# Delta rule prepared under the last projection units, its rows broadcast through DRAM, memory attention woven into the chunk steps

## The reference, cut to what matters

```python
h = rms_norm(x, mix_norm[l]) @ a_w_in[i]
qkv, gate, b_raw, a_raw, q_mem = jnp.split(h, ...)
o_a = gated_deltanet(qkv, gate, b_raw, a_raw, ...)        # 6 heads of 128
o_m = memory_attention(q_mem, mem_n @ w_mem_kv[l])        # 4 heads of 64, 256 keys
x = x + jnp.concatenate([o_a, o_m], axis=-1) @ w_out[l]
# inside gated_deltanet, after conv + silu and the l2 norms of q and k:
g_cum = cumsum(g)                                         # per chunk, per head
decay = exp(g_cum[i] - g_cum[j]) where j <= i
t_mat = where(strict, (k * beta) @ k.T * decay, 0) + eye
u = solve(t_mat, v * beta);  w = solve(t_mat, k * beta * exp(g_cum))
qk = (q @ k.T) * decay
# then chunk after chunk:
v_new = u_c - w_c @ state
out = q_c @ state + qk_c @ v_new
state = state * d_c + k_c.T @ v_new
```

## Time and profile before

| | us |
|---|---|
| median of three runs | 1333.41 (1329.31 to 1335.06) |
| profiled execution | 1335.27 |
| its span | 1333.1 |
| PE busy in the span | 1278.9 (96%) |
| DVE busy | 889.4 (67%) |
| ACT busy | 710.4 (53%) |
| POOL busy | 83.8 (6%) |

### The profile page before, as it was taken

One profiled execution on the slowest core, in us unless ns is written; L12 is line 12 of the kernel. 1 busy time (PEld: TensorE's weight loads), 2 busy tenths in 40 slices (PEclk: granted clock), 3 DMA queues, 4 the chain that ended last, 5 costly groups with the idle time before them and its releaser, 6 DMA issues.

```text
span 1333.1 us, 26311 instructions
## 1 busy us (share of the span) xinstructions
PE 1278.9 (96%) x10172; PEld 1244.6 (93%) x10172; DVE 889.4 (67%) x1503; ACT 710.4 (53%) x1026; POOL 83.8 (6%) x88
## 2 busy tenths in 40 slices
PE   7999999999999999899999999799999899999997
PEld 7899999999999987898999999699999868999996
DVE  7576689766657966436766755766665666766644
ACT  6445656666546762344666544556544444756432
POOL 7270000000000000430000000000000000000000
PEclk9999999999999997698999999899999998999999
DMA  8535555555644431002555642455564312555630
GB/s 329 187 105 195 168 180 190 190 189 191 227 153 160 160 129 61 1 1 66 187 189 189 233 178 94 151 180 180 200 235 150 107 64 96 186 178 182 242 126 32
DMA packets 48396, 208.71 MB, mean 157 GB/s; under 512 B 3376, under 2 KB 5560, under 8 KB 43848
## 3 DMA queue, kind: packets, MB, share of 16 engines
q1 hardware_dynamic: 46992, 203.89, 44.2%
q10 hardware_dynamic: 1336, 3.89, 0.8%
HBM read 206.68 MB, written 1.09 MB: 156 GB/s over the span
## 4 chain that ended last, share of the span: by engine, by line
PE 90%; DVE 5%; ACT 2%; issue 2%; DMA 0%; POOL 0%; ACTq 0%; DVEq 0%
PE main L1591 27%; PE main L1593 27%; PE main L1592 27%; PE main L1963 3%; PE side L1673 1%; DVE w_lo L823 1%; PE main L1948 1%; PE side L1653 1%; PE side L2004 1%; PE main L1933 1%; PE side L1684 0%; PE main L1934 0%; PE main L2018 0%; PE side L1641 0%; ACT w_hi L447 0%
## 5 line engine op out<-in xcount | busy, mean ns | idle before, releaser
L1591 PE MATMUL main<-xg_hi,w_hi 128*128 128x256 f32 (+1 forms) x2024 | 573.2, 283 | 2.5 <-DVE w_lo L823 0.9
L1592 PE MATMUL main<-xg_hi,w_lo 128*128 128x256 f32 (+1 forms) x2024 | 570.9, 282 | 0.0
L1593 PE MATMUL main<-xg_lo,w_hi 128*128 128x256 f32 (+1 forms) x2024 | 570.5, 282 | 0.0
L447 ACT ACTIVATE w_hi<-raw 128x1024 fp32r<-128x1024 f32 (+2 forms) x364 | 404.6, 1114 | 302.9 <-PE main L1593 300.5
L823 DVE TENSOR_TENSOR w_lo<-raw,w_hi 128x1024 fp32r<-128x1024 f32 (+2 forms) x364 | 466.4, 1288 | 6.3 <-ACT w_hi L447 5.5
L1591 PEld LDWEIGHTS main<-xg_hi,w_hi 128*128 128x128 f32 x2024 | 383.3, 189 | 5.8 <-issue 1.7
L1593 PEld LDWEIGHTS main<-xg_lo,w_hi 128*128 128x128 f32 x2024 | 383.9, 190 | 0.0
L1592 PEld LDWEIGHTS main<-xg_hi,w_lo 128*128 128x128 f32 x2024 | 381.0, 188 | 0.5
L1591 PE MATMUL main<-h_hi,w_hi 128*128 128x256 f32 x704 | 198.1, 281 | 0.0
L1592 PE MATMUL main<-h_hi,w_lo 128*128 128x256 f32 x704 | 198.1, 281 | 0.0
L1593 PE MATMUL main<-h_lo,w_hi 128*128 128x256 f32 x704 | 198.1, 281 | 0.0
(11 more groups left out here) (360 smaller groups left out, 1516.1 us busy)
## 6 DMA issues: line engine op xcount, KB each, us to landing
raw<-in_w_gu_a SPq DMA_DIRECT2D x44, 1024.0 KB, 5.2
raw<-in_w_gu_b SPq DMA_DIRECT2D x44, 1024.0 KB, 5.2
raw<-in_w_down_a SPq DMA_DIRECT2D x16, 1408.0 KB, 5.8
raw<-in_w_down_b SPq DMA_DIRECT2D x16, 1408.0 KB, 5.9
raw<-in_w_in SPq DMA_DIRECT2D x20, 1024.0 KB, 5.3
raw<-in_w_in_a SPq DMA_DIRECT2D x13, 1024.0 KB, 5.2
raw<-in_w_up SPq DMA_DIRECT2D x4, 1024.0 KB, 5.1
raw<-in_w_out SPq DMA_DIRECT2D x4, 1024.0 KB, 5.2
```

What stands on the lines that cost most here:

```text
L447: act.activation(w_hi[:, u % RING, 0:n], raw[:, s % RAW, u % 2, 0:n], ACT.Copy).then_inc(hi_ready, 1)
L1591: pe.matmul(dst, a_hi, b_hi, start=first, stop=False)
L1592: pe.matmul(dst, a_lo, b_hi, start=False, stop=False)
L1593: return pe.matmul(dst, a_hi, b_lo, start=False, stop=last)
```

## The change

It does five things.

- `ba` is projected after turn 1; its Sigmoid, Exp and Ln lie in turns 3 and 4 of ScalarE, the scan in turn 6 of VectorE, its transpose in turn 7 of TensorE, the Sqrt of the norms in turn 15, the column scales in turn 16 of VectorE, with the turn into rows right behind unit 16 on TensorE.
- The 24 rows go to DRAM from ScalarE's queue in turn 17 and come back in turn 18 and after, 512 KB for each head, broadcast over the partitions (`spread_rows`), in place of `along_rows`.
- The grams of head h are made after unit 18 + h, into two side banks in turn. VectorE makes the decay of head h in turn 19 + h (`decays`) and `n_t`, `a_t` in turn 20 + h (`grams`); GpSimd multiplies by the broadcast rows.
- v is turned in turns 20 to 22 and scaled by ScalarE, k in turns 24 and 25.
- The four memory heads leave the projection loop and stand between the sets of the recurrence.

The products of the inversion, the streams of weights and everything outside layer A's mixer are unchanged. The diff, cut to these parts:

```diff
 # ScalarE
+                if t == 3:
+                    act.wait_ge(evac, BA_TILE + 1)
+                    act.activation(ba[0:6, :], ba[0:6, :], ACT.Sigmoid).then_inc(ba_act, 1)
+                    act.wait_ge(ba_dve, 1)
+                    link(act.activation(sp2[32:38, :], sp1[32:38, :], ACT.Abs))
+                if t == 4:
+                    act.activation(small[32:38, 30:31], par[32:38, C_ALOG:C_ALOG + 1], ACT.Exp).then_inc(ba_act, 1)
+                    link(act.activation(sp2[32:38, :], sp2[32:38, :], ACT.Exp, scale=-1.0))
+                    act.activation(sp2[32:38, :], sp2[32:38, :], ACT.Ln, bias=one_c[32:38, :]).then_inc(ba_act, 1)
...
+                if t == 15:
                     act.wait_ge(csum, 12)
...
+                if t == 17:
+                    act.wait_ge(rows_ready, 1)
+                    act.dma_start(delta_rows.rearrange("h (i n) -> (h i) n", i=4), head_rows[:, :]).then_inc(rows_out, 16)
+                if t == 18:
+                    act.wait_ge(rows_out, 16)
+                    for h in range(3):
+                        spread_rows(h)
+                if t >= 19 and t - 19 < DH:
+                    h = t - 19
+                    act.wait_ge(diff_ready, h + 1)
+                    act.activation(dec[:, h % 2, 0, :], dec[:, h % 2, 0, :], ACT.Exp).then_inc(decay_ready, 1)
+                    if 0 <= h - 1 and h + 2 < DH:
+                        act.wait_ge(dec_ready, h)
+                        spread_rows(h + 2)
+                if t >= 21 and t - 21 < 3:
+                    j = t - 21
+                    act.wait_ge(turned_v, j + 1)
+                    for i in range(4):
+                        h, c = 2 * j + i // 2, i % 2
+                        ins = act.activation(kqv[:, 12 + h, c * P:(c + 1) * P], side[2][:, i * P:(i + 1) * P],
+                                             ACT.Copy, scale=b_col[:, c, h:h + 1])
...
+            exps(MEM_A)
+            new_values(vn0, 0, 1)
+            new_values(vn0, 1, 2)
+            exps(MEM_A + 1)
+            copy_pt(MEM_A)
+            act.wait_ge(rec_dve, 4)
+            square_outputs(0)
+            exps(MEM_A + 2)
+            copy_pt(MEM_A + 1)
+            new_values(vn1, 0, 9)
+            new_values(vn1, 1, 10)
+            exps(MEM_A + 3)
+            copy_pt(MEM_A + 2)
             act.wait_ge(rec_dve, 12)
...
 # VectorE
             link(dve.memset(cx[:, :, 0:3], 0.0))
+            dve.wait_ge(small_hi, 2)
+            low(wba_lo[:, :], wba[:, :], wba_hi[:, :]).then_inc(small_lo, 1)
+
+            def decays(h):
+
+                r, d = h % 3, h % 2
+                dve.wait_ge(spread_in[r], 16 * (h // 3 + 1))
+                for c in range(2):
+                    dve.scalar_tensor_tensor(dec[:, d, 0, c * P:(c + 1) * P], spread[:, r, 1, c * P:(c + 1) * P],
+                                             g_col[:, c, h:h + 1], const[:, K_CAUS:K_CAUS + P],
+                                             ALU.subtract, ALU.add)
+                dve.tensor_tensor(g_last[:, h:h + 1], spread[:, r, 1, P - 1:P], g_col[:, 0, h:h + 1],
+                                  ALU.subtract).then_inc(diff_ready, 1)
+
+            def grams(h):
+
+                dve.wait_ge(dec_ready, h + 1)
+                dve.wait_ge(gram, h + 1)
+                for i, dst in enumerate((n_t, a_t)):
+                    for c in range(2):
+                        ins = dve.scalar_tensor_tensor(
+                            dst[:, 2 * h + c, :], side[h % 2][:, i * SEQ + c * P:i * SEQ + (c + 1) * P],
+                            kq_inv[:, c, h:h + 1], dec[:, h % 2, 1 + i, c * P:(c + 1) * P], ALU.mult, ALU.mult)
+                ins.then_inc(n_ready, 1)
 
             def convolve(t, taps):
...
+                if t == 16:
+                    dve.wait_ge(col_act, 2)
+                    link(dve.reciprocal(cols[:, 80:104], cols[:, 184:208]))
+                    k_beta, q_scale = packed[:, :, :, 0], packed[:, :, :, 2]
+                    dve.tensor_tensor(k_beta, kq_inv[:, :, 0:6], b_col, ALU.mult)
+                    dve.tensor_copy(packed[:, :, :, 1], g_col)
+                    link(dve.tensor_scalar(q_scale, kq_inv[:, :, 6:12], DK ** -0.5, None, ALU.mult))
+                    dve.tensor_tensor(packed[:, :, :, 3], q_scale, e_g, ALU.mult).then_inc(cpk_ready, 1)
+                    link(dve.tensor_tensor(k_neg, k_beta, e_g, ALU.mult))
+                    dve.tensor_scalar(k_neg, k_neg, -1.0, None, ALU.mult)
+                if t == 17:
+                    dve.wait_ge(rows_t, 1)
+                    dve.tensor_copy(head_rows[:, :], side[3][0:24, 256:512]).then_inc(rows_ready, 1)
+                if t >= 19 and t - 19 < DH:
+                    decays(t - 19)
+                if t >= 20:
+                    grams(t - 20)
+
...
+            row_maxima(MEM_A)
+            row_maxima(MEM_A + 1)
+            normalise(MEM_A)
+            for j in range(2):
+                by_heads(state, main[2 + j], j, 3 + j)
+            normalise(MEM_A + 1)
+            for j in range(2):
+                by_heads(o_a[:, :, 0:P], main[j], j, 5 + j)
+            row_maxima(MEM_A + 2)
...
 # GpSimd
+            for h in range(DH):
+                r, d = h % 3, h % 2
+                gp.wait_ge(decay_ready, h + 1)
+                if h >= 2:
+                    gp.wait_ge(n_ready, h - 1)
+                gp.tensor_tensor(dec[:, d, 1, :], dec[:, d, 0, :], spread[:, r, 0, :], ALU.mult)
+                gp.tensor_tensor(dec[:, d, 2, :], dec[:, d, 0, :], spread[:, r, 2, :], ALU.mult)
+                gp.wait_ge(gram, h + 1)
+                q_late = kqv[:, 6 + h, P:SEQ]
+                gp.tensor_tensor(q_late, q_late, spread[:, r, 3, P:SEQ], ALU.mult).then_inc(dec_ready, 1)
...
 # TensorE
+                if t == 1:
+
+                    bank = bank_of(BA_TILE)
+                    pe.wait_ge(small_lo, 2)
+                    for k in range(KC):
+                        w = slice(k * 38, k * 38 + P)
+                        ins = triple(bank[:, 0:SEQ], wba_hi[:, w], wba_lo[:, w], xs_hi[:, k], xs_lo[:, k],
+                                     k == 0, k == KC - 1)
+                    ins.then_inc(extra_done, 1)
                 if 3 <= t < 15:
...
+                if t == 7:
                     pe.wait_ge(ba_dve, 2)
...
+                if t == 16:
                     pe.wait_ge(cpk_ready, 1)
...
+                if t >= 18 and t - 18 < DH:
+
+                    h = t - 18
+                    if h >= 2:
+                        pe.wait_ge(n_ready, h - 1)
+                    for i, other in enumerate((h, 6 + h)):
+                        for c in range(2):
+                            ins = pe.matmul(side[h % 2][:, (2 * i + c) * P:(2 * i + c + 1) * P], kqv[:, h, chunks[c]],
+                                            kqv[:, other, chunks[c]], start=True, stop=True)
+                    ins.then_inc(gram, 1)
+                if t >= 20 and t - 20 < 3:
+
+                    j = t - 20
+                    if j == 0:
+                        pe.wait_ge(csilu, 18)
+                    else:
+                        pe.wait_ge(vt_done, j)
+                    for i in range(4):
+                        ins = pe.transpose(side[2][:, i * P:(i + 1) * P],
+                                           kqv[:, 12 + 2 * j + i // 2, i % 2 * P:(i % 2 + 1) * P], ident)
+                    ins.then_inc(turned_v, 1)
+                if t >= 24:
+
+                    j = t - 24
+                    pe.wait_ge(vt_done, 3)
+                    for i in range(3):
+                        ins = pe.transpose(side[2 + j][:, i * P:(i + 1) * P], kqv[:, 3 * j + i, 0:P], ident)
+                    ins.then_inc(turned_k, 1)
 
...
             pe.wait_ge(ident_ready, 1)
-            pe.wait_ge(rows_ready, 1)
-            chunks = (slice(0, P), slice(P, SEQ))
-            for h in range(DH):
-                for i, (r0, r1) in enumerate(((h, 6 + h), (12 + h, 18 + h))):
-                    bank = bank_of(t0 + 3 * h + i)
-                    along_rows(bank[:, 0:SEQ], r0)
-                    along_rows(bank[:, SEQ:2 * SEQ], r1).then_inc(spread, 1)
-                bank = bank_of(t0 + 3 * h + 2)
-                for i, other in enumerate((h, 6 + h)):
-                    for c in range(2):
-                        ins = pe.matmul(bank[:, (2 * i + c) * P:(2 * i + c + 1) * P], kqv[:, h, chunks[c]],
-                                        kqv[:, other, chunks[c]], start=True, stop=True)
-                ins.then_inc(gram, 1)
-            t0 = FIRST_TILE["kt"]
-            for j, (a, b) in enumerate(((0, 4), (4, 6))):
-                bank = bank_of(t0 + j)
...
 
-            pe.wait_ge(d_dve, 21)
-
-            each(main[0:2], [(lambda h: d_t[:, h, :], lambda h: kqv[:, 12 + h, 0:P])])
-
-            each(main[2:4], [(lambda h: k_dec[:, h, :], lambda h: vn0[:, h, :])],
+            scores(MEM_A)
+            scores(MEM_A + 1)
+
```

(31 more changed lines are left out.)

312 lines of the change are left out of this document (113 added, 199 removed).

## The result

The changed kernel takes 1347.7 us (median of four runs, 1345.22 to 1350.54) against 1331.83 us for the kernel before on the same chip: ratio 1.0119, 95% interval 1.0086 to 1.0151. It is slower, as forecast (1342; the range 1324 to 1356 holds it). The profiled execution is 1345.22 us (span 1343.4), 9.95 us above that of before; the medians lie 15.9 us apart.

The account below looks back on a forecast made before the run. TensorE's chain of waits was taken to bound the kernel. Removing 44.0 us and adding 34.0 under the projection, 8.5 in the recurrence and 10.4 for the clock gave +8.9: 1344.2 against the profile, 1342 against the median; range 1324 to 1356.

Parts of the forecast that it names:

- (c): Turn 1 of the projection: TensorE waits for `wba_lo`, made by VectorE behind a reciprocal; 1.4 us, between 0 and 2.4.
- (d): Turn 7: TensorE waits for the scan, late through ScalarE's five function switches; 4.4 us, and 0.3 for the transpose.
- (e): Turn 16: TensorE waits right behind unit 16 for VectorE's column scales; 4.3 us with the two transposes.
- (g): Turns 21 to 23: before each gram TensorE waits for VectorE's `n_ready` of head h - 2; 3.3 us each, 9.9 us.
- (h): Turn 20: TensorE's wait includes the DMA of the broadcast rows, taken as 4 us; 5.0 us, from 3.3 to 9.
- (i): Between the last unit and the inversion's first product: 8.5 us where 7.5 stood, 1.0 us more, from 0 to 3.
- (j): Recurrence: scores, transposes and outputs of the four memory heads, less filled idle time, plus new waits; 8.5 us added.
- (k): Low TensorE clock after the gaps of turns 7, 16 and 20 to 24: 10.4 us added, bounds 0 and 18.
- the rival's 2.66: ScalarE function switch costs load plus drain, 2.66 us; the rival has turn 7 wait 6.4 us longer, 1348, chance 0.03.
- The rival with the clock at 1.00: The clock holds in the projection's gaps, so (k) falls: 1333 us, chance 0.24.
- (a): Memory attention leaves turns 21 to 25 of the projection: 16.3 us of 30.5 removed.
- (b): From 514.89 to 542.55, turn of v, column scales, rows, head loop and turn of k go: 27.7 us removed.

Follow-up runs that it names:

- the repeat: The changed kernel itself, unaltered, timed again beside later runs on one chip: 1346.93 us, 1.0096 of the kernel before.

## Why the prediction held, and which steps missed

Step by step, against the first profile of the change:

| step | forecast | read |
|---|---|---|
| (c) `wba_lo` | 1.4 | 1.28 |
| (d) unit 7 | 4.4 + 0.3 | 3.74 + 0.97, and the transposes |
| (e) unit 16 | 4.3 with transposes | 3.89, and the transposes |
| (g) units 21 to 23 | 3 x 3.3 | 3 x 3.28 |
| (h) unit 20 | 5.0 | 7.10 |
| (i) lead-in | +1.0 | +2.5 |
| (j) recurrence | +8.5 | +8.66 from first product to squares, +9.4 behind the inversion |
| (k) clock | +10.4 (0 to 18) | 7.7 ahead of the lead-in here, 15.6 in the repeat |
| first product | 0 to 8 before 550.04 | 1.4 behind it |

**Right.** The waits behind a unit (c, d, e, g) were read from VectorE's and ScalarE's work between `unit_done` and the semaphore, and came within about 0.3 us each. In (d) TensorE stood first for `csq` of the late ScalarE (L1946), a wait that I had not named, and only 0.97 for the scan. The lateness was there (4.24 us on VectorE), so the price behind unit 7 was close to the 4.4, 4.71. The scan itself came 5.7 us behind unit 7, and the sums of `csq` filled 1.0 of it. The switch cost its load alone; of the rival's 2.66 only the 1.28 was seen. The figure of the Trainium skill (ScalarE: Activation LUTs, What ACT_TABLE_LOAD costs) is met by the trace in its load and not in its drain.

**Missed: (h).** I assumed that 512 KB land in 4 us. VectorE could start 6.2 us after the issue (496.09 to 502.28), three broadcasts and a slab of weights being under way. That is 2.2 us; the issue came 0.6 sooner than I had it. Whether the other transfers or the size alone made it late stays open, since the run with the broadcasts one by one didn't separate the first two. From there to the end of head 0's grams I had 4.6 us and 5.1 passed (502.28 to 507.4), GpSimd's first product taking twice its time. **Missed: (i).** The unit's end to the first product is 10.0 us (541.45 to 551.42), I had 8.5: GpSimd's last product of head 5 took 1.44 us beside VectorE's split (0.49 otherwise), and the mask waited for it: 0.95 of the 1.5 us.

**Missed by a little: (j).** From the end of the inversion's products to the squares are 9.4 us more (12.3 before, less its 0.78 of idle time; 591.46 to 613.16 now), above the 8 to 9 of the forecast. TensorE's work for the four heads was less than the 10.2 forecast, by 0.8, since the first pair's scores ran side by side. The waits were more: 1.34 and 0.69, 2.0 in all, where 1.2 stood in the sum and 0.7 was taken off again. The +8.66 looks nearer because the inversion's first 16 records cost 0.7 less clock here than before (2.68 against 3.37 us from start to start).

With what was read, the sum up to the first product is -44.0 + 1.3 + 5.0 + 4.4 + 7.7 + 9.8 + 7.1 + 2.5 + 7.7 = +1.5 us (f as forecast), and +1.4 was read.

**(k), right as a mechanism and wide in size.** By the clock records, in the first profile 15.4 us of TensorE's busy time between 440 us and the inversion ran at the lower level, 7.7 us lost; in the repeat (the profile at 1351.86 us) 31.2, so 15.6. At the inversion's start 4.7 and 5.9 more ran low. The turns that begin at gram 3 and gram 4 are the example: 7.71 and 9.30 us in the first, 10.28 and 10.26 in the repeat. The eight runs of the change follow the mean granted clock of their span: 1345.22 us at 0.974, 1347.5 and 1347.9 at 0.971, 1350.54 at 0.968, and in the repeat 1346.05 and 1346.21 at 0.973, 1347.64 at 0.971, 1351.86 at 0.967. The first profile was the fastest of its four, and the profile of before a slow one of its kind, which is why the medians lie 14 to 16 us apart where the first profiles lie 10. Filling the gaps gave 7.1 back. The rival with the clock at 1.00 stood at 1333 (by its own sum, 1342 less 10.4, it is 1332); held there by filler the kernel takes 1339.9, since what (h), (i) and (j) had too low remains (2.1, 1.5 and 0.9 us), the one low stretch left costs 1.7, and that behind the squares is longer than before the change (11.4 us busy in it against 9.4, 1.0 us lost, which no step of the sum had). Together that is 7.2 of the 7.9 us.

**Luck in the number.** In the first profiles +10.0 stands against the forecast's +8.9. There (h) and (i) were 3.6 us too low and (k) 2.7 too high, and they nearly cancel. The medians, at a typical clock, are 15.9 us apart (13.9 with the repeat), 5 to 7 above the forecast. The direction wasn't luck: less the 3.6 us of (h) and (i), the first profile would still lie some 6 us above that of before.

**(a) and (j) as a pair.** In the sum they are 16.3 and 8.5. Alone on the chip they are 9.7 and 9.98: zero. The 16.3 assumed that the scan and the scales are not late, which the other edits see to. Here the steps priced from the trace held for the full change, not for one of them alone.

**The unnamed cause.** I took the waits of (g) as VectorE's work within a unit and priced them right, but didn't ask why a gram had to wait for the one two before it. One more bank and one moved turn of v gave 20 us.

**A reading that doesn't hold.** The prediction says that TensorE ran the old head loop "behind VectorE's pace". The row has TensorE busy 22.26 of 22.40 us and VectorE 16.23, so TensorE, at a clock of 0.50, was the full one. No term rests on it, since (b) takes the whole stretch away.

## What to carry to other kernels

When work of another engine is slipped under a stream of matmuls, the price is not its duration but every place where the in-order engine meets a result begun by the unit just ended. Count those places, and give each result a buffer or a turn more: here four such moves, with no operation removed, turned 1.2% slower into 1.3% faster. Price what a wait does to the clock beside the wait: a gap of 3.28 us cost up to 2.57 more.
